# Router logits of a mixture-of-experts layer: tokens as the stationary operand, sixteen weight columns moving

## What is computed

```python
h2 = modulate(rmsnorm(x, norm_ffn[l]), sh2, sc2)                  # (512, 1024)
scores = sigmoid(einsum('bsd,de->bse', h2, router_w))             # (512, 16), the router logits
sel = scores + router_bias
...                                                               # best group of 4 experts, best 2 experts in it
w = take_along_axis(scores, e_idx, -1);  w = w / sum(w)
...                                                               # the experts, weighed by w
```

## Time and profile before

| what | value |
|---|---|
| median of three runs | 2244.61 us (2240.77 to 2245.73) |
| the profiled execution, its own time | 2246.07 us |
| its span in the profile | 2244.3 us |
| TensorE (PE) matmuls busy | 2129.4 us, 95% of the span |
| VectorE (DVE), ScalarE (ACT), GpSimd (POOL) busy | 66%, 45%, 17% |

### The profile page before, as it was taken

How to read it: one execution, slowest core, us unless ns; L and a number is a source line. 1 busy time by engine, 2 the same in 40 slices (tenths; PEclk the granted TensorE clock), 3 DMA queues, 4 the chain that set the end, 5 groups by cost and what they waited for, 6 DMA issues and landing times.

```text
span 2244.3 us, 32746 instructions
## 1 busy us (share of the span) xinstructions
PE 2129.4 (95%) x12051; PEld 1707.2 (76%) x12051; DVE 1483.5 (66%) x2695; ACT 1010.8 (45%) x1867; POOL 377.3 (17%) x346
## 2 busy tenths in 40 slices
PE   8999999999899999999999999999998989999996
PEld 5897788787687786777679978888966878777774
DVE  4737766655767876777646477666467688377775
ACT  4523334554565324555435333345445644445551
POOL 2002200000001431354300021000000024124441
PEclk9999999999999999999999999999999999999998
DMA  9332233241325665766642223333222267546653
GB/s 313 94 88 62 81 118 94 76 120 57 91 91 199 242 240 211 277 253 244 193 150 88 81 81 91 102 112 96 78 69 80 87 234 269 203 165 241 244 210 120
DMA packets 196573, 333.71 MB, mean 149 GB/s; under 512 B 30528, under 2 KB 153280, under 8 KB 180416
## 3 DMA queue, kind: packets, MB, share of 16 engines
q1 hardware_dynamic: 169184, 305.33, 40.1%
q0 software_dynamic: 19296, 19.98, 2.8%
q10 hardware_dynamic: 7936, 6.30, 0.9%
HBM read 352.48 MB, written 51.38 MB: 180 GB/s over the span
## 4 chain that ended last, share of the span: by engine, by line
PE 75%; DVE 11%; ACT 5%; issue 3%; DMA 3%; POOL 0%; SPq 0%; POOLq 0%; DVEq 0%; ACTq 0%
PE ps L874 70%; PE ps L872 6%; DVE spare L2088 2%; DVE ring_rounded L2106 2%; ACT WH_rounded L1587 2%; DMA SQKV<-gate_logits 1%; DMA DVt<-gate_logits 1%; DVE nmax L2343 1%; DMA Y<-y_rows 1%; DVE SC L2716 0%; DVE ps L2340 0%; DVE ssq L2273 0%; POOL M L3058 0%; DVE SC L2366 0%; DVE SQKV L2284 0%
## 5 line engine op out<-in xcount | busy, mean ns | idle before, releaser
L874 PE MATMUL ps<-X_rounded,WH_rounded 128*128 128x512 f32 x768 | 341.0, 444 | 15.9 <-DVE ring_rounded L2106 4.5
L2106 DVE TENSOR_TENSOR ring_rounded<-ring,WH_rounded 128x512 fp32r<-128x512 f32 (+2 forms) x190 | 235.0, 1245 | 134.0 <-ACT WH_rounded L1587 133.6
L874 PE MATMUL ps<-H_rounded,WH_rounded 128*128 128x512 f32 x768 | 302.9, 394 | 8.7 <-DVE SC L2716 8.7
L874 PE MATMUL ps<-X_rounded,ring_rounded 128*128 128x512 f32 x768 | 302.6, 394 | 0.0
L874 PE MATMUL ps<-WH_rounded,X_rounded 128*128 128x256 f32 (+1 forms) x960 | 275.1, 287 | 3.1 <-ACT M L1879 1.0
L874 PE MATMUL ps<-ring_rounded,X_rounded 128*128 128x256 f32 (+1 forms) x960 | 271.6, 283 | 0.0
L874 PE MATMUL ps<-WH_rounded,H_rounded 128*128 128x256 f32 (+1 forms) x960 | 271.4, 283 | 0.0
L3058 POOL TENSOR_TENSOR M<-M,SC 128x512 f32<-128x512 f32 x48 | 75.7, 1590 | 961.4 <-DVE SC L2716 961.4
L1587 ACT ACTIVATE WH_rounded<-ring 128x512 fp32r<-128x512 f32 (+2 forms) x190 | 195.1, 1036 | 75.2 <-PE ps L874 63.1
L874 PEld LDWEIGHTS ps<-X_rounded,WH_rounded 128*128 128x128 f32 x768 | 145.5, 189 | 68.8 <-issue 27.4
L874 PEld LDWEIGHTS ps<-WH_rounded,X_rounded 128*128 128x128 f32 x960 | 184.6, 192 | 5.3 <-issue 2.4
(11 more groups left out here) (399 smaller groups left out, 4492.1 us busy)
## 6 DMA issues: line engine op xcount, KB each, us to landing
ring<-in_w_in SPq DMA_DIRECT2D x272, 256.0 KB, 4.0
Y<-in_moe_w_down SPq DMA_DIRECT2D x18, 1024.0 KB, 6.7
ring<-in_ada_w SPq DMA_DIRECT2D x64, 256.0 KB, 4.6
ring<-in_w_branch SPq DMA_DIRECT2D x64, 256.0 KB, 5.1
TM<-in_ada_w SPq DMA_DIRECT2D x14, 1024.0 KB, 10.5
DQK<-in_ada_w SPq DMA_DIRECT2D x14, 1024.0 KB, 9.4
ring<-in_moe_w_down SPq DMA_DIRECT2D x14, 1024.0 KB, 6.2
gate_logits<-CM SPq DMA_DIRECT2D x44, 256.0 KB, 2.8
```

The source lines that it names most:

```text
L874: ins = nc.tensor.matmul(o, lhsT, rhs, start=start, stop=stop)
L2106: ins = v.tensor_tensor(low[j][:, at:at + size], ring[:, j, at:at + size], high[i][:, at:at + size].bitcast(F32), ALU.subtract)
```

## The change

The logits are computed the other way round. For each feature chunk k the kernel now issues four matmuls, one for each token tile t: the stationary operand is `H[:, k, tt(t)]`, 128 features by 128 tokens, and the moving operand is `rw[:, k]`, 16 columns. The four tiles have 16 columns each in bank 6, with 128 tokens on the partitions. So ScalarE's sigmoid writes `rt[:, 0]` at once, the turn of the scores, its bank 7 and the copy fall away, and `handed[6]` takes the place of `handed[7]`. The four tiles of token rows follow one another. `warm(5, 5)` ahead of the logits becomes `warm(1, 5)`: one filler matmul of two passes in place of five of ten.

```diff
-        scores_T = SC[0:NE, 3]
...
-                warm(5, 5)
+                warm(1, 5)
                 free(6)
                 eng.wait_ge(params_loaded, p.next(params_loaded, param_count(l)))
                 alone()
                 for k in range(NC):
                     eng.wait_ge(h_ready, p.next(h_ready))
-                    ins = mm(ps[0:NE, 6], rw[:, k], H[:, k], k == 0, k == NC - 1, last=k == NC - 1)
+                    for t in range(NT):
+                        ins = mm(ps[:, 6, t * NE:(t + 1) * NE], H[:, k, tt(t)], rw[:, k], (k, t) == (0, 0), (k, t) == (NC - 1, NT - 1),
+                                 last=k == NC - 1)
                 ins.then_inc(filled[6], p.gives(filled[6]))
-                p.mark(emptied[6])
+                p.mark(handed[6])
...
-                token_rows(0)
-                free(6)
-                free(7)
-                alone()
                 for t in range(NT):
-                    ins = turn(ps[:, 7, t * NE:(t + 1) * NE], scores_T[:, tt(t)], k=NE, last=t == NT - 1)
-                ins.then_inc(filled[7], p.gives(filled[7]))
-                p.mark(handed[7])
-                for t in range(1, NT):
                     token_rows(t)
...
-                act(scores_T, ps[0:NE, 6], ACT.Sigmoid).then_inc(emptied[6], p.gives(emptied[6]))
+                act(rt[:, 0], bank(6, NT * NE), ACT.Sigmoid).then_inc(handed[6], p.gives(handed[6]))
...
-                token_rows(0)
-                eng.wait_ge(filled[7], p.next(filled[7]))
-                act(rt[:, 0], bank(7, NT * NE), ACT.Copy).then_inc(handed[7], p.gives(handed[7]))
-                for t in range(1, NT):
+                for t in range(NT):
                     token_rows(t)
...
-                p.mark(filled[7])
-                eng.wait_ge(handed[7], p.next(handed[7]))
+                eng.wait_ge(handed[6], p.next(handed[6]))
```

## The result

| | kernel before | changed kernel |
|---|---|---|
| median | 2245.17 us (4 runs, 2240.77 to 2246.09) | 2262.87 us (4 runs, 2257.36 to 2264.96) |
| profiled execution, its span | 2246.07, 2244.3 us | 2264.96, 2263.2 us |
| PE, PEld busy | 2129.4, 1707.2 us | 2142.8, 1731.1 us |

The ratio is 1.0074, with a 95% interval of 1.0061 to 1.0087: 17.7 us slower by the medians. The forecast was slower, by 12.6, with a median of 2257.2; the measured one lies just inside the upper edge of its range, 2263.

A forecast was written before the change was run, and what follows sets the result against it. TensorE, 95% busy, was taken as the bound. Layer 0 +5.5 and layer 1 +7.1 gave +12.6 on the profiled 2246.07: 2258.7, or 2257.2 us for the median, that execution being 1.5 above it; range 2250 to 2263, extended to 2247.

The forecast's parts named there:

- Rival A: Both layers' 64 logit records: the clock holds, not slower; -1.75 and -0.45 us, time 2242.4; chance 0.12.
- Rival B: Logits: weight loads hide better, so `h_ready` sets the pace; -5.0 and -2.5 us, time 2237; chance 0.02.
- Rival C: Logits: clock falls late in one layer, or low-clock loads take 0.107 us; +4 to +7, about 2250; chance 0.06.
- Layer 0's logits: 64 records at 0.213 us, 13.65 us, starting 2.4 us earlier at 842.2 and ending 4.3 us later, at 855.85.
- as before: Layer 0 ahead of the logits: clock already low from 840.8, and without the ten fillers nothing brings it back.
- Layer 1's: Logits start unchanged at 1949.42; 7 records at 0.107 us, 57 at 0.213, together 12.9 us, ending 5.9 later.
- The turns: 32 turns of token rows behind the logits: 4 us of low clock, 6.2 us in all, 1.2 more than now.
- The fillers: Nine filler matmuls behind the turns: stay 18 passes, 3.9 us at 2.4 GHz; TensorE reaches the count 3 us after `routed`.
- To the count: Sum up to the count of tokens: +5.5 us in layer 0, +7.1 in layer 1, together +12.6.
- taken as nothing: Low-clock stretches after the count, moved by 5 to 7 us: up to 1.5 us more or less per layer, counted as zero.

The follow-up runs named there:

- first form with 128: Changed kernel with 128 moving columns, 3 filler matmuls ahead of the logits and 5 behind the turns; 2243.98 us, ratio 0.9995 against the kernel before.
- second profile: Profile from running the changed kernel again, unaltered; 2260.78 us (6 runs), ratio 1.0067 against the kernel before.

## Why the prediction was right

**Direction and mechanism: right.** The clock is 0.50 through most of the 64 records, the records are 0.21 us apart there, and TensorE reaches the count 3.4 and 3.0 us after VectorE's choice. Rival A was wrong because with 16 columns, and even with 64, the clock does not hold. Rival B did not come up: loads at 1.00 stay 0.10 to 0.11 us apart, with all the rest ready. Rival C stood for a single layer; both fell in both profiles.

**Layer 0's logits** were forecast at 5.97 us after the norm (2.4 earlier, as seen) for 13.65; measured 12.72 and 13.67. The prediction had the clock low from 840.8 on, "as before". That step was partly wrong: in the first profile it was 1.00 at the start and fell near 848.1, 1.1 us into the logits (0.87 on average over 847.10 to 848.50). What it rested on, that a run of one-column matmuls is followed by a fall, holds in three places of the kernel before (behind the third of them stand six filler passes from 1498.32 on, which the earlier trace rows leave out, before the clock falls at 1499.5) and not in layer 0 of the kernel with the old logits and 1 filler, of the one with 96 columns, or of the first form with 128. **Layer 1's** were forecast at 12.9 us with a fall 0.7 us in; measured 13.11, fall at 1960.9, 0.65 us in, and 13.48. That the 0.7 us came out is luck: the fall stood 0.3 us in in the second profile and right at the start in the kernel with fewer fillers behind.

**The turns** were given 6.2 us with 4 us of low clock; measured 6.73 and 6.37, with 5.5 and 4.6 us of it. They did bring the clock back by themselves: the row at 859.80 holds nothing but turns, and from 865.3 on the clock reads 1.00. So the Trainium skill's statement, "TensorE: Matmul & The Clock Gate", Part 4, that transposes don't count, does not hold in this kernel, and the 2 us per layer that it would have added did not come. **The fillers** behind stayed at 3.88 us.

**To the count** this makes 5.0 and 7.5 us, 12.5, where the forecast had 5.5 and 7.1, 12.6. That the sum agrees to 0.1 is partly luck: layer 0's logits were 0.9 us shorter than forecast, and the turns 0.5 and 0.2 us and layer 1's logits 0.2 us longer.

**The step that was too small** is "taken as nothing" for the stretches behind the count. They took 0.3 us more in layer 0 and 1.3 in layer 1 (count to gather 20.62 instead of 19.32), inside the 1.5 that the prediction allowed. It is the same clock: in layer 1 it is low from 1995.1 to 2001.9 for the last matmuls ahead of the gather, where the kernel before had it low from 1977.5 to 1980.9.

That makes 14.1 us (15.0 in the second profile). The medians say 17.7 and 16.3. What is left, 1 to 4 us, is not settled. One part of it can be argued, not shown: the profiled execution of the kernel before had a fall ahead of layer 0's logits that cost 2.4 us, and its time was 2246.07, above its median, so the forecast may have started from an execution that was slower there than most. Measured from the 83.9 us of the old logits with 1 filler instead, which had no such fall, the changed kernel's two profiles are 16.2 and 17.1 us longer.

## What to carry to other kernels

Swapping operands so that a full activation tile is stationary and a narrow weight matrix moves costs the same count of array time on paper (64 x 0.107 against 16 x 0.43 us), but it turns a stretch of streaming into a stretch of weight loads. If such a stretch is several us long on the critical path, read PEclk over it before the sum is made: here it halved the clock, nearly doubled the stretch (6.97 to 12.7 and more) and made the turns behind it 1.3 to 1.7 us longer. Work that computes nothing, copies of the moving columns here, can be free or better (eight copies took back 11 to 13 us), and fillers placed to meet another engine must be counted again when either side moves.

## What was not expected

- Streaming eight times as many columns made the stage faster: 2249.4 us with 128 columns against 2260.8 to 2262.9 with 16, and the jump lay between 64 columns (2261.6) and 96 (2248.8); no width between them was run.
- The clock fell at 848.0 in the kernel with five fillers with TensorE and its weight loads busy for all of the 3.1 us before it. The Trainium skill, "TensorE: Matmul & The Clock Gate", in its table on why this matters, names only idle gaps as what throttles; the run shows that a stretch without one can.
- A gap of 2.7 us ahead of the old, wide logits cost nothing in the kernel with one filler (clock 1.00), while a gap of 1.9 us ahead of 128-column logits was followed by a fall at 1951.0, 1.1 us into them, in another. Where a fall comes differs between executions of the same code by several us: layer 0's norm moved by 7 us over eleven profiles.
